# Reordering the end of a trunk kernel's mixers: modulation transposes, early expert weights, and the projection tail of layer 1

## The reference

```
sh1, sc1, g1, sh2, sc2, g2 = adaln(cond, p['w_ada'], p['b_ada'])
h = rms_norm(x, p['g_norm1']) * (1 + sc1) + sh1
y, state = mixer(h, p, rope, ctx)
x = x + g1 * y
h = rms_norm(x, p['g_norm2']) * (1 + sc2) + sh2
x = x + g2 * hier_moe(h, p)
```

## Time and profile before

| | us |
|---|---|
| median of 3 runs | 998.84 |
| lowest, highest run | 997.6, 1000.68 |
| the profiled execution | 998.84 |
| its span in the profile | 997.0 |
| PE busy | 892.1 (89%) |
| DVE busy | 407.8 (41%) |
| ACT busy | 239.9 (24%) |
| POOL busy | 120.3 (12%) |
| bytes moved | 318.83 MB, mean 320 GB/s |

### The profile page before, as it was taken

How to read it: one execution, slowest core, us unless ns; L and a number is a source line. 1 busy time by engine, 2 the same in 40 slices (tenths; PEclk the granted TensorE clock), 3 DMA queues, 4 the chain that set the end, 5 groups by cost and what they waited for, 6 DMA issues and landing times.

```text
span 997.0 us, 14444 instructions
## 1 busy us (share of the span) xinstructions
PE 892.1 (89%) x5445; PEld 493.7 (50%) x5445; DVE 407.8 (41%) x1190; ACT 239.9 (24%) x604; POOL 120.3 (12%) x131
## 2 busy tenths in 40 slices
PE   4999889998999997998799998998979999889880
PEld 2445436546455554555366564554655555445440
DVE  2102376347522251311364665563763222522114
ACT  3111144111111111111344455333211111111111
POOL 1000000100122221221100000001002222212210
PEclk9999999999999999999999999999999999999996
DMA  9989799738899999999950039607699999999965
GB/s 374 398 328 404 290 421 416 258 140 348 329 418 417 409 417 366 417 418 363 329 202 7 1 107 370 252 1 216 234 421 379 418 418 409 416 374 417 418 277 196
DMA packets 61683, 318.83 MB, mean 320 GB/s; under 512 B 12598, under 2 KB 13878, under 8 KB 31528
## 3 DMA queue, kind: packets, MB, share of 16 engines
q1 hardware_dynamic: 46144, 285.84, 71.1%
q0 software_dynamic: 13328, 25.02, 7.4%
q10 hardware_dynamic: 2144, 7.06, 1.8%
HBM read 312.72 MB, written 26.49 MB: 340 GB/s over the span
## 4 chain that ended last, share of the span: by engine, by line
PE 69%; DMA 15%; DVE 10%; issue 2%; ACT 2%; SPq 1%; POOL 0%; POOLq 0%; DVEq 0%; ACTq 0%
PE psum L915 19%; PE psum L928 9%; DMA ring<-in_l_w 8%; PE psum L1121 7%; PE psum L1233 3%; PE psum L851 3%; PE psum L864 3%; PE psum L895 2%; PE psum L1242 2%; PE psum L695 2%; DMA scratch<-token_rows_hbm,overflow_rows 2%; DMA ring<-in_l_w_ada 2%; PE psum L921 2%; PE psum L1325 1%; DMA ring<-in_ada_first 1%
## 5 line engine op out<-in xcount | busy, mean ns | idle before, releaser
L915 PE MATMUL psum<-ring,scratch 128*64 128x256 f32 x1744 | 208.5, 391 | 16.7 <-DMA ring<-in_l_w 15.1
L915 PEld LDWEIGHTS psum<-ring,scratch 128*64 128x64 f32 x1744 | 129.6, 140 | 80.0 <-issue 25.7
L2236 DVE TENSOR_TENSOR scratch<-scratch,psum 64x256 f32<-64x256 f32 x64 | 27.2, 425 | 282.2 <-ACT scratch L1517 282.1
L928 PE MATMUL psum<-ring,scratch 128*64 128x512 f32 x464 | 112.2, 604 | 2.6 <-ACT scratch L1521 1.9
L2697 POOL DMA_INDIRECT expert_rows<-scratch,slot_rows x64 | 63.7, 995 | 318.5 <-ACT scratch L1531 318.5
L1517 ACT ACTIVATE scratch<-psum 64x256 f32<-64x256 f32 x64 | 24.0, 375 | 245.3 <-PE psum L915 245.3
L1121 PE MATMUL psum<-ring,scratch 128*128 128x512 f32 x192 | 73.5, 540 | 1.5 <-DVE scratch L1847 1.5
L1531 ACT COPY scratch<-psum 128x512 f32<-128x512 f32 x64 | 37.5, 586 | 134.7 <-PE psum L928 132.1
L1121 PEld LDWEIGHTS psum<-ring,scratch 128*128 128x128 f32 x192 | 36.0, 190 | 36.6 <-issue 35.5
L928 PEld LDWEIGHTS psum<-ring,scratch 128*64 128x64 f32 x464 | 29.1, 136 | 42.3 <-issue 37.2
L2218 DVE COPY scratch<-psum 128x512 f32<-128x512 f32 x64 | 41.4, 687 | 7.1 <-PE psum L877 6.2
(11 more groups left out here) (384 smaller groups left out, 1218.0 us busy)
## 6 DMA issues: line engine op xcount, KB each, us to landing
ring<-in_l_w SPq DMA_DIRECT2D x108, 1024.0 KB, 16.7
ring<-in_l_w_rows SPq DMA_DIRECT2D x56, 1024.0 KB, 14.9
ring<-in_l_w_ada SPq DMA_DIRECT2D x40, 1024.0 KB, 12.2
ring<-in_ada_first SPq DMA_DIRECT2D x8, 1024.0 KB, 16.0
ring<-in_l_w_o SPq DMA_DIRECT2D x8, 1024.0 KB, 14.3
ring<-in_l_w_in SPq DMA_DIRECT2D x4, 1024.0 KB, 22.0
gate_rows<-gate_rows_hbm POOLq DMA_DIRECT2D x8, 512.0 KB, 8.5
scale_shift<-gate_rows_hbm POOLq DMA_DIRECT2D x8, 512.0 KB, 10.6
```

The costliest lines, as they stand in the source:

```text
L915: last = nc.tensor.matmul(ps[64 * n:64 * n + 64, 2 + par, 0:DE], mine[:, k, :], part(w, k * DE, DE), start=k == 0, stop=k == KD - 1)
L928: last = nc.tensor.matmul(ps[64 * n:64 * n + 64, 5 + par, :], hhT[:, par, k, :], part(w2, k * D + n * 512, 512), start=k == 0, stop=k == 1)
```

## The change

Nothing is computed otherwise; these are the parts.

1. **Order of layer 1's loads.** `first` becomes expert 0's three matrices, then expert 2's `w1` and `w3`, then expert 1's three, then expert 2's `w2` and expert 3's. Expert 0's `w1` now waits until all 20 score steps are done, and all three matrices of expert 1 wait for the whole projection.
2. **Expert 4's `w2`** is loaded later, in both layers: after expert 4's `w3` and no longer among the experts 0 to 3.
3. **Layer 1's modulation columns** are transposed in layer 0's router, and their biases are added in `route_blocks(0)`, both out of layer 0's mixer.
4. **Layer 1's projection tail.** PE transposes tile 0 ahead of `project_last(1, 0)`; DVE does `scaled(1, 0)` and `norm(3, 0)` ahead of `residual_sample`, and `norm(3, 1)` ahead of `residual_last`. ACT copies tile 0's transposes out before it squares tile 1.
5. Two scratch places move (`scaled_of`, `tmp`), and `transpose_scaled` loses its wait on `mod_ready`.

```diff
                 if l:
-                    first = first[6:8] + first[0:3] + first[5:6] + first[8:] + first[3:5]
+                    first = first[0:3] + first[6:8] + first[3:6] + first[8:]
                 for u, n in first:
-                    if (u, n) == ((2, 0) if l else (2, 2)):
+                    if (u, n) == ((0, 0) if l else (2, 2)):
...
-                        if l:
-                            sp.wait_ge(S["down_done"], AGAIN[0] + 1)
-                        sp.wait_ge(S["modT_in_psum"], 3)
-                        sp.wait_ge(S["shift_in_psum"], 1)
-                        sp.wait_ge(S["m_out"], 32)
-                        load_matrix(l, block_of(EARLY[0]), 2, early[EARLY[0]][2][0]).then_inc(S["early_in"], 16)
                     unit = U_MOE[l] + 3 * u + n
+                    if l and u == 0 and n == 0:
+                        sp.wait_ge(S["scores_in_psum"], len(MIX0) + len(ATT1))
                     if l and (u, n) in ((2, 0), (2, 1)):
                         sp.wait_ge(S["ada_used"], KD)
-                    if l and u == 0:
-                        sp.wait_ge(S["scores_in_psum"], len(MIX0) + (len(ATT1) if n else 4))
-                    if l and (u, n) == (1, 2):
-                        sp.wait_ge(S["att_in_psum"], len(MIX0) + len(ATT1))
-                    if l and (u, n) in ((1, 0), (1, 1)):
+                    if l and u == 1:
                         sp.wait_ge(S["units_used"], used(U_WO[1] + 3))
...
                 load_matrix(l, block_of(four), 1, early[four][1][0]).then_inc(S["early_in"], 16)
+                sp.wait_ge(S["modT_in_psum"], 3)
+                sp.wait_ge(S["m_out"], 32 * (l + 1))
+                load_matrix(l, block_of(four), 2, early[four][2][0]).then_inc(S["early_in"], 16)
...
+                if l == 0:
+                    transpose_modulation(1, 5)
                 keep_running(4, 3)
...
             transpose_shift(0, 2)
-            transpose_modulation(1, 3)
             out_projection(1)
...
             project_first_sample()
+            transpose_scaled(1, 0)
             pe.wait_ge(S["att_ready"], len(MIX0) + len(ATT1))
             project_last(1, 0)
-            transpose_scaled(1, 0)
             transpose_scaled(1, 1)
...
             put_state(1, 0)
+            evac_h(3, h2T, 0)
             rms(3, (1,))
             put_state(1, 1)
-            evac_h(3, h2T, 0)
...
             def route_blocks(l):
 
+                if l == 0:
+                    modulation_columns(1, 5)
...
             shift_products(1, 7)
+            scaled(1, 0)
+            norm(3, 0)
             residual_sample()
-            scaled(1, 0)
+            evac_h(3, h2T, 0)
             scaled(1, 1)
+            norm(3, 1)
             residual_last(1)
```

More of the change, by code:

```diff
@@ L311, in qk, with scaled_of @@
             return view(W, qk_at[t % 2], QKW)
-        def scaled_of(l, t):
-            return view(W, (9088, 6144 if l else 8192, 5120)[t], D)
+        def scaled_of(t):
+            return view(W, (9088, 8192, 5120)[t], D)
         shiftT = view(W, 10112, 2, 2, 4)
@@ L745, in transpose_scaled @@
                     pe.wait_ge(S["shift_ready"], l + 1)
-                    pe.wait_ge(S["mod_ready"], 3)
                 for k in range(KD):
                     last = nc.tensor.transpose(ps[:, h_bank(2 * l + 1, t) + k // 4, k % 4 * P:(k % 4 + 1) * P],
-                                               scaled_of(l, t)[:, k * P:(k + 1) * P], ident)
+                                               scaled_of(t)[:, k * P:(k + 1) * P], ident)
                 last.then_inc(S["hT_in_psum"], 1)
@@ L1871, in norm @@
                 V.scalar_tensor_tensor(out=hp[:, t, :, :].rearrange("p k q -> p q k"),
-                                       in0=scaled_of(l, t).rearrange("p (q k) -> p q k", k=KD), scalar=ss[:, 8 + t:9 + t],
+                                       in0=scaled_of(t).rearrange("p (q k) -> p q k", k=KD), scalar=ss[:, 8 + t:9 + t],
                                        in1=b.rearrange("p (q k) -> p q k", k=KD),
@@ L1880, in scaled @@
                 c = cond_of(t)
-                V.tensor_tensor(scaled_of(l, t), x[:, t, :], AB[:, c * D:(c + 1) * D], ALU.mult).then_inc(S["xa_ready"], 1)
+                V.tensor_tensor(scaled_of(t), x[:, t, :], AB[:, c * D:(c + 1) * D], ALU.mult).then_inc(S["xa_ready"], 1)
             def residual_last(l):
@@ L1890, in residual_last @@
                     part = slice(hf * 512, (hf + 1) * 512)
-                    tmp = view(W, 7168, 512)
+                    tmp = view(W, 9216, 512)
                     link(V.tensor_tensor(tmp, ps[:, 4 + hf, :], G[:, 1, part], ALU.mult))
@@ L1895, in residual_last @@
                     dve.wait_ge(done, count)
-                    last = V.tensor_tensor(scaled_of(l, 2)[:, part], x[:, 2, part], AB[:, D + hf * 512:D + (hf + 1) * 512],
+                    last = V.tensor_tensor(scaled_of(2)[:, part], x[:, 2, part], AB[:, D + hf * 512:D + (hf + 1) * 512],
                                            ALU.mult)
                     if hf == 0:
[L1899 to L1903, removed]
+                        evac_h(2 * l + 1, h2T, 1)
                 last.then_inc(S["xa_ready"], 1)
@@ L2437, in _ @@
             shift_products(0, 2)
-            modulation_columns(1, 3)
             residual(1, 1)
```

## The result

The changed kernel takes 1010.19 us (median of 4 runs, 1009.53 to 1014.45) where the kernel before takes 998.31 in the same comparison: ratio 1.014, 95% interval 1.011 to 1.0169. It is **slower**, by 1.4%: the medians lie 11.9 us apart, the ratio, which rests on more runs, gives 14.0 (11.0 to 16.9). The forecast was 1016.4 us, range 1008 to 1020. The profiled execution took 1012.09 us with a span of 1010.3, 13.3 us longer than the span before (997.0).

What follows compares the result with a forecast made beforehand. The prediction took the DMA queue's weight loads to bound layer 1's experts. PE's tail 9.25, queue terms 8.35 (5.6 + 5.0 - 2.25) and layer 0's 0 made 17.6 us on 998.8: 1016.4 us, range 1008 to 1020.

Steps and rivals of the forecast that it cites:

- The first gated issue: Layer 1's loads on SP: first issue after the projection at 714.00 instead of 708.42 us, +5.6 us plus PE's lateness.
- PE's tail: Layer 1's projection: PE late by 7.65 us waiting for modulation rows and 1.6 us of clock, +9.25 us.
- The stall: Layer 1's projection: PE waits for `scaled(1, 0)` before tile 0's transposes, 4.15 us, or 7.65 with rows landing late.
- the clock: Layer 1's projection: PE's clock falls after its wait, costing 1.6 us, between 0 and 1.8.
- The later landing: Before layer 1's projection: added loads from 677.3 us push the modulation rows' landing back 3.5 us, bounds 0 and 5.0.
- Two matrices into the flow: Layer 1's full queue: `w2` of experts 1 and 4 add 5.0 us; queue idle used up gives back 2.25.
- PE's pace: Rival on layer 1's experts: PE sets their pace, so only its 9.25 us delay counts, 1008.1 us; chance 0.07.
- The signs: Expected in the new profile: five loads at 677.3 us, PE idle about 7.6 us, no queue dip at 745 to 755.
- One sign of being wrong: Layer 1's experts: the prediction is wrong if experts 0 to 15 wait for weights.
- Layer 0, net 0: Layer 0: -0.43 us on PE, +0.40 on DVE, expert 4's `w2` covered by idle queue; net 0 within 0.5 us.
- The rule weighed: Last modulation matrices: removing a load queued behind them gives PE's waits nothing back, 0 us; 1.5 us kept as bound.

Runs made afterwards that it cites:

- e5: The changed kernel itself, run again beside the kernel before on one chip; ratio 1.0092, +9.2 us.
- e2: Kernel before with only the new order of layer 1's loads and expert 4's late `w2`; ratio 1.0039, +3.9 us.
- e3: Kernel before with only the new order of layer 1's loads; ratio 1.0026, +2.6 us.
- e7: Changed kernel with expert 2's `w2` and expert 3 issued ahead of expert 1; ratio to the kernel before 1.0055, +5.5 us.
- e1: Kernel before with only the changed projection tail of layer 1 and its scratch places, loads as before; ratio 1.0074, +7.4 us.
- e10: Kernel before with only layer 1's modulation columns moved into layer 0's router; ratio 1.0016, +1.6 us.
- e8: Kernel before with `norm(3, 0)` and `norm(3, 1)` moved ahead of DVE's last residual, so POOL's row stores go earlier; ratio 0.9991, -0.9 us.
- e11: Kernel before with 64 of 2048 columns loaded of layer 1's `w2` of experts 2 and 3, 2 MB less; ratio 1.0002, +0.2 us.
- e12: Kernel before with 64 of 2048 columns loaded of layer 1's `w2` of experts 8 and 9, 2 MB less; ratio 0.998, -2.0 us.
- e6: Changed kernel with 13 filler matmuls on PE ahead of tile 0's transposes; ratio to the kernel before 1.0127, +12.7 us.
- e9: Changed kernel with 6 filler matmuls on PE ahead of tile 0's transposes; ratio to the kernel before 1.011, +11.0 us.
- e4: Kernel before with only expert 4's `w2` loaded later, in both layers; ratio 1.0012, +1.2 us.

## Why the prediction was right, and where its sum was off

Direction and range held, and the mechanism in the main; the sum was 17.6 us, and the change costs 11.9 by the medians and 14.0 by the ratio (9.2 in e5). By the trace, counted from S, the end of the weights moved by 290.21 - 278.54 = 11.7 us (e5: 9.1): 13.2 up to G, where the forecast had 14.85, and -1.6 from G on, where it had +2.75. The rest of the 13.3 us of span is S, 3.2 us later, less 1.6 us behind E, where the last up products took 3.67 us and before 5.36, at a granted clock of 0.68.

- **The first gated issue, +5.6:** right, measured 5.15. In e2 and e3 G - S is 5.15 us later with PE's tail unchanged, and e7 takes it back.
- **PE's tail, +9.25:** right in kind, somewhat large. The projection ends 8.1 us later after S in the first profile, 5.3 in e5, 5.3 in e1. The stall was 6.01 us (7.65 forecast), the clock 1.95 (1.6).
- **The later landing, +3.5:** too large. `scaled` starts 18.73 us after S, before 16.79, so +1.9, and +1.0 in e5. In e1, whose loads stayed in place, it came at 16.29: the loads at 677 us do push the rows back, by less than their added queue time. The forecast read the share of 0.90 as a queue with 1.5 us of room. From S to the landing it had more, before (first row) and after (second):

```profile
684.05:700.84 16.79, 16.79 (x41) 7.52 (x40) 5.07 (x9) 1.74 (x6) 2.86 (x4) 1.00 0.81 220
687.24:705.97 18.73, 14.00 (x34) 5.99 (x32) 2.62 (x7) 1.38 (x4) 2.85 (x4) 0.95 0.91 305
```

  That is 3.7 MB in 16.79 us and 5.7 MB in 18.73. The two added megabytes took 1.9 us more, since a share of 0.81 at 220 GB/s left room that the share alone does not tell.
- **Two matrices into the flow, +5.0, less 2.25 of idle:** this is the step that failed. From G to E the changed kernel needs 252.6 us, the kernel before 254.2: 1.6 less, not 2.75 more. Summed over windows of 2.5 us, 103.13 MB moved in that stretch and 102.55 before, +0.6 and not +2.1. The sum had missed that POOL's two row stores of 0.5 MB, which stood in the flow before, are issued at 709.61 and 716.10 us now, ahead of G, where the queue has room: about -2.5 us, an estimate from 1.05 MB at 0.419. Idle fell by 1.7 us in those windows (6.4 to 4.7), not by 2.25. With 1.4 us for the 0.6 MB this makes -0.3 us, so 1.3 of the 1.6 us stay unexplained.
- **What both terms left out** is the gate path. The kernel before ends by it (E - R = 212.16), 1.8 us behind its queue path. So the first 1.8 us of queue delay are free, which the forecast did have, as the idle of 1.6 us. But a later tail of PE also counts by R alone, with no load moved. In e1 the sum would give 9.25 - 3.5 = 5.75, and R - S went up by 3.8 and E - S by 3.9; my written expectation of +1 to +3 for it was wrong. R - S moved less than the tail (5.25) because the first gather took 2.94 us there and 4.33 before; with the gather equally fast, as in e3 and e4 (R - S 65.0), the step is 5.2. Some 3.5 us of e1's +7.4 stand in no trace. For the change itself the queue path decides: the gate path would end 72.99 + 212.1 = 285.1 us after S, and E is at 290.2.
- **PE's pace** as a rival was half right: PE's tail reaches the end by R, not because PE outruns the weights. Its 1008.1 us was nearer than the forecast's 1016.4 to the measured 1010.2.
- **The signs:** five ring loads from 680.47 us on, the stall, the missing dip at 745 to 755 and none of the expert loads between projection start and end came as written. One sign of being wrong came too, by 0.84 us: expert 15 waits for its weights, where the forecast had the first wait near 16 or 17. PE's lead over the queue was used up sooner than forecast, although the queue itself was less late.
- **Layer 0, net 0:** part 3 gives 0.4 us in the mixer, as forecast (SP's first load behind it goes out at 218.36 us, before at 218.78). That nothing else is lost needs part 2 beside it, which I had not seen (e10). S was 3.2 us later in both profiles of the change, but with layer 0 as in the kernel before it lies anywhere from 684.05 to 689.51 (before, e1, e3, e8, e11, e12), and in the other traces with the changed layer 0 (e6, e7, e9) from 684.56 to 690.99, so the runs don't show a loss there.
- **The rule weighed** (no gain at the last modulation matrices): PE's waits there are 3.0 us in three pieces after the change too, as the earlier trace rows. The Trainium skill ("DMA: Bandwidth & Descriptors", section "Two DMAs through the same engine are not ordered") says that the descriptors of one queue of a DMA engine start in order. The forecast took from this that a load behind gives nothing back when it leaves, and the trace agrees, with 3.0 us again.

What stays open: the time of e9 against e5, and e8's true value, are inside the intervals of about 0.25 to 0.3%, and the 5 us between the change's two comparisons (+14.0 and +9.2, whose intervals just overlap) were not explained; their traces differ by 2.6. A version that beats the kernel before was not found.

## What to carry to other kernels

Where a DMA queue and an engine hand the lead to each other, look for a pause of the queue in the flow and ask what ends it: work taken away ahead of such a gate only makes the pause longer, and a delay of the engine that opens the gate went to the end in full in these traces. When an edit delays the start of a flow, count what else slips out of the flow into the gap, the small stores of other queues as well. And when a load is gated by a semaphore, list the loads that stand behind it on the same engine, since moving the signal moves them all. Before a DMA share is read as a full queue, read the GB/s beside it.

## What the runs showed of the hardware

- **The same PE code differs by microseconds in where the low clock falls.** With the low stretch in the filler matmuls (L762 in before) the first gather is fast, otherwise slow. From the traces of e4 (granted clock 0.66 from 725 to 730 us) and e8 (0.50 from 734 to 739):

```profile
725.98 5.38 PE L759 MATMUL psum<-constants 128*128 128x512 f32 x8
734.72 2.94 PE L874 MATMUL psum<-scratch 128*128 128x128 f32 x24 [1.15 <-DVE scratch L2030]
```
```profile
725.65 3.68 PE L762 MATMUL psum<-constants 128*128 128x512 f32 x8
734.39 5.49 PE L877 MATMUL psum<-scratch 128*128 128x128 f32 x24 [1.15 <-DVE scratch L2030]
```

  The fillers end in an idle stretch anyway, the gather is on the gate path: R - S is 65.0 in e3 and e4, and 69.1 to 69.5 in e8, e11 and e12. Where the queue pauses at R, E - S follows R - S one to one (278.54 at 66.38, 281.51 at 69.47), so up to 3 us of it go to the end. Of the traces with PE's tail unchanged the gather took 2.94 us in three (e3, e4, e10) and 4.33 to 5.49 in the other five; with the changed tail and its stall it took 2.94 in all four (change, e1, e5, e7), with the stall filled 4.43 and 5.49. Whether the stall causes this was not tested.
- **A 128 x 512 filler counts twice:** `keep_running(13, 4)` shows 26 records and 11.32 us, so two records and 0.87 us for each of the 13 matmuls, where I had taken 0.46.
- In e1 the read-back of the experts' rows at the end took 8.53 us of the chain, before 4.16, for no cause that the trace names.
